# Selected-value pages of three samples issued from ScalarE's DMA queue in place of GpSimd's

## The reference

```
nsa_past = cache_nsa_kv[l, page_table].reshape(bs, past_len, 4, HEAD_DIM)
moba_past = cache_moba_kv[l, page_table].reshape(bs, past_len, 2, H_MOBA, HEAD_DIM)
...
o_sel = jnp.einsum('bqhjs,bqjsd->bqhd', p2.reshape(sc.shape).astype(q.dtype), vg)
```

## Time and profile before

| | us |
|---|---|
| median of 3 runs | 775.93 (774.74 to 780.44) |
| profiled execution, its own time | 781.36 |
| its span | 779.7 |
| PE busy | 738.0 (95%) |
| DVE busy | 433.2 (56%) |
| ACT busy | 286.1 (37%) |
| POOL busy | 196.9 (25%) |

### The profile page before, as it was taken

One profiled execution on the slowest core, in us unless ns is written; L12 is line 12 of the kernel. 1 busy time (PEld: TensorE's weight loads), 2 busy tenths in 40 slices (PEclk: granted clock), 3 DMA queues, 4 the chain that ended last, 5 costly groups with the idle time before them and its releaser, 6 DMA issues.

```text
span 779.7 us, 17384 instructions
## 1 busy us (share of the span) xinstructions
PE 738.0 (95%) x6888; PEld 657.0 (84%) x6888; DVE 433.2 (56%) x748; ACT 286.1 (37%) x560; POOL 196.9 (25%) x265
## 2 busy tenths in 40 slices
PE   9999999988977999899999999999999999999994
PEld 8999989765544455479989999999999999999994
DVE  4878984655543542455866556524553346536356
ACT  5232234544534322442434554212432123314125
POOL 0000636002333554002837732000210011100433
PEclk9999999989997999999999999999999999999998
DMA  9656772458887787422243323332323223335002
GB/s 333 183 153 181 201 211 82 187 196 308 276 304 271 231 247 230 155 63 74 82 162 97 95 82 108 109 107 67 100 82 108 86 78 106 93 100 162 2 15 96
DMA packets 65772, 113.47 MB, mean 146 GB/s; under 512 B 19066, under 2 KB 38267, under 8 KB 65019
## 3 DMA queue, kind: packets, MB, share of 16 engines
q1 hardware_dynamic: 59674, 96.11, 39.8%
q0 software_dynamic: 6016, 16.26, 6.0%
HBM read 107.90 MB, written 6.52 MB: 147 GB/s over the span
## 4 chain that ended last, share of the span: by engine, by line
PE 75%; DVE 10%; issue 5%; ACT 4%; SPq 3%; DMA 3%; POOL 0%; POOLq 0%; ACTq 0%; DVEq 0%
PE psum L779 53%; PE psum L798 4%; PE psum L806 3%; SPq L696 2%; DMA moba_hi<-in_moba_pages 2%; PE psum L885 2%; PE psum L854 2%; PE psum L1084 2%; PE psum L919 2%; PE psum L1072 1%; DVE wL L1596 1%; DVE yc L1666 1%; DMA wgate<-in_w_gate 1%; DVE oxL L2025 1%; ACT wH L1236 1%
## 5 line engine op out<-in xcount | busy, mean ns | idle before, releaser
L1596 DVE TENSOR_TENSOR wL<-raw,wH 128x1024 fp32r<-128x1024 f32 (+1 forms) x87 | 109.5, 1260 | 87.6 <-ACT wH L1236 87.6
L1236 ACT ACTIVATE wH<-raw 128x1024 fp32r<-128x1024 f32 (+1 forms) x87 | 88.8, 1021 | 102.9 <-PE psum L779 100.7
L779 PE MATMUL psum<-oxH,wH 128*128 128x260 f32 (+1 forms) x512 | 105.0, 286 | 1.5 <-DVE wL L1596 0.9
L779 PE MATMUL psum<-oxH,wL 128*128 128x260 f32 (+1 forms) x512 | 103.8, 284 | 0.0
L779 PE MATMUL psum<-oxL,wH 128*128 128x260 f32 (+1 forms) x512 | 103.4, 283 | 0.0
L779 PE MATMUL psum<-opH,wH 128*128 128x260 f32 x400 | 86.1, 297 | 4.0 <-DVE wL L1596 1.4
L1560 POOL TENSOR_TENSOR hsq<-relu 128x520 f32<-128x520 f32 x32 | 33.7, 1054 | 218.7 <-ACT relu L1415 218.7
L779 PEld LDWEIGHTS psum<-oxH,wH 128*128 128x128 f32 x512 | 79.5, 189 | 3.4 <-issue 2.5
L779 PE MATMUL psum<-opH,wL 128*128 128x260 f32 x400 | 81.0, 284 | 0.0
L779 PE MATMUL psum<-opL,wH 128*128 128x260 f32 x400 | 81.0, 284 | 0.0
L779 PEld LDWEIGHTS psum<-oxL,wH 128*128 128x128 f32 x512 | 79.9, 190 | 0.0
(11 more groups left out here) (386 smaller groups left out, 1297.3 us busy)
## 6 DMA issues: line engine op xcount, KB each, us to landing
raw<-in_panels SPq DMA_DIRECT2D x88, 512.0 KB, 3.6
nsa_ring<-in_nsa_pages SPq DMA_DIRECT2D x128, 96.0 KB, 2.2
moba_hi<-in_moba_pages SPq DMA_DIRECT2D x36, 256.0 KB, 5.3
moba_lo<-in_moba_pages SPq DMA_DIRECT2D x36, 256.0 KB, 4.9
moba_lo<-in_moba_pages POOLq DMA_DIRECT2D x28, 256.0 KB, 5.0
moba_hi<-in_moba_pages POOLq DMA_DIRECT2D x28, 256.0 KB, 5.2
selV<-in_selv_pages SPq DMA_DIRECT2D x80, 32.0 KB, 3.0
xres<-in_xT SPq DMA_DIRECT2D x8, 260.0 KB, 5.5
```

What stands on the lines that cost most here:

```text
L779: last = mm(out[:, hf, 0:cols], w, x[:, k, hf * HALF:hf * HALF + cols], start=(t == 0 and j == 0), stop=(t == KT - 1 and j == 2))
L1236: fn(wtiles(0, n).rearrange("p a b -> p (a b)")[:, cols], raw[:, n % NRAW, cols], ACT.Copy).then_inc(h_done, 1)
L1596: tt(wtiles(1, n).rearrange("p a b -> p (a b)")[:, cols], raw[:, n % NRAW, cols], wtiles(0, n).rearrange("p a b -> p (a b)")[:, cols].bitc ...
```

## The change

`SELV_POOL` becomes `SELV_ACT` with the same samples (1, 3, 5). The steps `selv` 4 to 7, 12 to 15 and 20 to 23 leave GpSimd's program and enter ScalarE's, at their place in `TL`, in the form SyncE uses (one load of four page numbers for four DMAs). The first of them waits for the page numbers and for the last input panel; the wait for a MoBA pair that GpSimd's version had is gone. GpSimd keeps MoBA's odd units in this stage.

```
-SELV_POOL = (1, 3, 5)
+SELV_ACT = (1, 3, 5)
...
-                elif kind == "selv" and n // 4 not in SELV_POOL:
+                elif kind == "selv" and n // 4 not in SELV_ACT:
...
+                elif kind == "selv" and n // 4 in SELV_ACT:
+                    if n == 4:
+                        act.wait_ge(ids_in, 16)
+                        act.wait_ge(mm_done, N_IN_PANELS)
+                    ids = nc.values_load_multi_w_load_instructions(page_ids[0:1, 4 * n:4 * n + 4], [mybir.EngineType.Activation])[1]
+                    for p, v in enumerate(ids, 4 * n):
+                        nc.scalar.dma_start(selV[p // PAGES][:, p % PAGES, :],
+                                            a["selv_pages"][bass.ds(v, 1)].rearrange("a p n -> (a p) n")).then_inc(selv_in[p // PAGES], 16)
...
-                if kind == "selv" and n // 4 in SELV_POOL:
-
-                    if n == 4:
-                        pool.wait_ge(mm_done, N_IN_PANELS)
-                    pool.wait_ge(mp_mm, MB1 + n // 6 - 1)
-                    for p in range(n * 4, n * 4 + 4):
-                        v = pool.value_load(page_ids[0:1, p:p + 1])
-                        pool.dma_start(selV[p // PAGES][:, p % PAGES, :],
-                                       a["selv_pages"][bass.ds(v, 1)].rearrange("a p n -> (a p) n")).then_inc(selv_in[p // PAGES], 16)
-                elif kind == "xsum":
+                if kind == "xsum":
```

## The result

| | us |
|---|---|
| median after, 4 runs | 809.24 (806.10 to 811.61) |
| median before, 4 runs | 775.93 (774.74 to 780.44) |
| ratio | 1.040 [1.037, 1.044] |
| profiled execution after, its span | 809.9 |

A forecast was written before the change was run, and what follows sets the result against it. TensorE, busy 95% of 779.7 us, was taken as the bound, held up by a late ScalarE in the attention stage. Stalls 26.6 plus clock 3.0 less 0 gave +29.6 on 775.9: 805.5 us, range 796 to 815.

The forecast's parts named there:

- The price of a group: ScalarE's time for one load of four page numbers and four DMAs, taken as 2.70 us; twelve groups added.
- q: Symbol for the time of one four-page group on ScalarE: 2.70 us, with 2.39 and 3.6 also worked through.
- The rival of cheap issue: Issuing costs ScalarE much less than SyncE (chance 0.15); a group at 1.0 to 2.0 us gives 784 to 794.
- not slower: Issues fit into ScalarE's idle gaps of 0.6 to 2.3 us, leaving the kernel not slower; chance 0.07.
- The four stalls: Delays behind ScalarE's four page blocks, after MoBA pairs 10 to 13, each block's time less slack; 26.6 us in all.
- The clock: TensorE's granted clock halves behind long stalls: 1.5 us each for stalls 3 and 4, bounds 0 and 1.7.
- stalls 3 and 4: Behind ScalarE's two blocks of 16 pages, at 271.59 and 280.82 us: delays of 9.9 and 9.4 us.
- stall 1: Behind ScalarE's first 8 pages, at 248.30 us: `shift` and TensorE's first score block late by 5.4 us, no slack.
- Stall 2: Behind ScalarE's second 8 pages, at 261.08 us: an exponential late, slack 3.5 us, delay 1.9 us.
- What comes back: Gain from GpSimd losing 48 page issues: put at 0, at most 4.2 us if SyncE's run became shorter.
- unit 31: MoBA unit whose issue moves up 14 us on GpSimd; its 1.10 us wait goes, taken back at sample 7.
- ScalarE and SyncE in each other's way: Rival, chance 0.23: the two engines hold each other up issuing together, adding 5 to 10 us, 810 to 815.

The follow-up runs named there:

- spread: Kernel after, but ScalarE issues the 48 pages as twelve single groups of four, each ahead of an activation it waited for before; 780.89 us, ratio 1.006.
- s1: Kernel after, but only sample 1's 16 pages on ScalarE (two blocks of 8), samples 3 and 5 on GpSimd; 787.31 us, ratio 1.010.
- s3: Kernel after, but only sample 3's 16 pages on ScalarE (one block), samples 1 and 5 on GpSimd; 791.09 us, ratio 1.015.
- s5: Kernel after, but only sample 5's 16 pages on ScalarE (one block), samples 1 and 3 on GpSimd; 794.98 us, ratio 1.017.
- pool024: Kernel after, with the pages of samples 0, 2 and 4 moved from SyncE to GpSimd; 808.70 us, ratio 1.044.

## Why the prediction was right, and where it was not

**The price of a group: right.** q = 2.70 us came from SyncE's rows. Twelve groups on ScalarE took 32.1 us where 32.4 were forecast, the four blocks 5.2, 5.5, 11.7 and 9.7 where it was 5.4, 5.4, 10.8 and 10.8. ScalarE's DMA instruction is 0.339 us at least, beside SyncE's 0.332. The rival of cheap issue, and with it that of "not slower", falls.

By the Trainium skill (DMA: Bandwidth & Descriptors, Issuing engines are not separate DMA queues) issuing from another engine saves only the sequencer's time, usually small beside the transfer; so the choice of engine would have left about 776 us. The runs disagree where the issues stand in front of work, 32.1 us of ScalarE for 48 pages, and are near it where they don't (spread, 780.9).

**The four stalls: right, one of them in part by luck.** 24.9 us against 26.6, at the four places: 5.3, 2.0, 9.3 and 8.3 where 5.4, 1.9, 9.9 and 9.4 were forecast. s1, s3 and s5 gave each its own cause. Gap less stall gives the slack: 0, 3.5 and 1.4 at the first, second and fourth, as forecast, but 11.7 - 9.3 = 2.4 at the third, where the prediction had 0.9. It had followed the chain over `Wt` and `Psel` to the transposes; TensorE stopped before that, at `cq` 7, until the exponential of `cq` 6 was done (9.25 <-ACT PT), and had no wait at the transposes. A block 0.9 us longer than forecast and a slack 1.5 us larger nearly cancel.

**The clock: right in kind, the term mis-sized.** "I take 1.5 for each, bounds 0 and 1.7", 3.0 us in all, was 8.7. Two statements failed. The bound was taken from a window of 3.4 us behind a wait of 3 us, as if half clock lasted about that long behind any stall. Behind the blocks it lasted 6.3, 3.5, 9.8 and 4.7 us, though TensorE had work nearly all the time, and behind stalls 3 and 4 it cost about 4.1 and 2.2 us, both over the bound of 1.7 (2.2 for each with one sample alone). And "stall 1 only lengthens a stall behind which the first matmuls are slow already" left out that the slow stretch can get longer too: 6 us where it was 3. Stall 2, of 1.9 us, was given no clock at all, and 274 to 277 ran at half clock behind it. The working had 26.6 + 3.0 - 0 = 29.6; the profiles show 24.9 + 8.7 - 1.4 = 32.2, and the medians differ by 33.3. The error of 5.7 us in this term is partly hidden by the two others. In another execution, pool024's, the same term was 5.0, so its size here is partly chance, and so is how near the sum came: the profiled spans differ by 30.2 us, since the profile of before was 2.2 us later at pair 10, and the medians by 33.3, 3.7 above the point.

**What comes back: small, but not nothing.** "both are unchanged but for unit 31" failed for SyncE's run, whose shortening the prediction had named as a sign of being wrong. It took 21.82 us in place of 23.21, so that the wait for sample 7 stayed near its length (2.94, forecast 4.2) and the piece from `spv` 2 to `spv` 7 became 1.4 us shorter. The run varies whatever GpSimd does, 21.3 to 22.7 in the runs with 32 pages above, and it was 21.8 in s1, where GpSimd still issued samples 3 and 5. So I can't say that GpSimd's silence shortened it; that before's profile shows a long one is as good a reading.

**ScalarE and SyncE in each other's way: false.** It had 0.23, and 5 to 10 us. pool024 puts it at 20 ns an instruction and no time in the whole. The single long instructions on which it rested (up to 1.7 us on ScalarE) come as well with SyncE quiet (up to 1.9).

The Trainium skill (Perfetto Trace Analysis, DMA Instruction — HWDGE (DVE, Sync)) tells of a generator locked in turn; the 20 ns may be that, which no run here shows, and here it is not worth more.

**Open.** What decides how long the clock stays down. It isn't the length of the stall alone: behind stalls of 8.75 (s3) and 9.25 us (after) it came back after some 5 and 9.8 us, and pool024, with 9.27, had it back after some 6.5. Nor is it the number of blocks, which is four in pool024 as in the full change. Whether several executions of one kernel differ as much as these kernels do isn't shown, since each has one profile. What interrupts single DMA instructions for 1 to 2 us is open as well.

## What to carry to other kernels

A DMA issue is an instruction of its engine, here 32.1 / 48 = 0.67 us for a page with a computed address, and a block of them costs what the engine's next result is late, however empty the engine is on average. Cut such a block into groups no longer than the engine's own waits and put them ahead of instructions that wait anyway: the same 48 issues cost 33 us in four blocks and about 4 (2 to 6) in twelve groups. And count a stall of TensorE of several microseconds as more than itself: here 24.9 us of stalls brought 8.7 us of slower matmuls in one profile, and 25.8 us of them brought 5.0 in another, so give that term a wide range.

## What the hardware showed that I had not expected

- The granted clock stayed at 0.50 for 9.8 us behind the third stall although TensorE was busy in 10.23 of the 10.9 us from 291.00.
- Whether it falls at all varied: it fell behind a stall of 1.90 us in the full change, and not behind one of 1.55 in s1; behind the first wait of 1.57 us it was half in before and full in s3 (1.92 and 1.05 us for the same matmuls).
- The same 1.58 MB went in 6912 packets by ScalarE's queue (144 a page) and in 1536 by GpSimd's (6016 - 4480, 32 a page). SyncE's queue takes 144 a page too (in pool024, which takes 48 pages off it, it has 59674 - 52762 = 6912 fewer). The packets under 512 B rose from 19066 to 25209, and in the kernel after no wait of TensorE for a transfer was longer than before.
- Single DMA instructions of 1.0 to 1.9 us turn up on ScalarE and on SyncE, with or without the other beside them, against a median of 0.34 to 0.36.
